# Hybrid decoder block on one core: a time mixer whose small matrix products are gathered into six runs a period in place of eight

## The chip, the core and the metric

The kernel runs on one core of a Trainium2 chip. Its engines run by themselves and meet only at semaphores: TensorE (PE, matrix products), VectorE (DVE), ScalarE (ACT), GpSimd (POOL), and SyncE (SP), which here only issues transfers. Each engine takes its instructions in the order in which they were written. The metric is the device time of one execution in microseconds; lower is better.

## What is computed

A decoder block on 256 tokens and 16 meta tokens, width 2048. One of its two token mixers is RWKV-7: 32 heads of 64, with a state S of 64x64 per head that runs over the tokens.

```
p = h @ w_in
r, k, v, wl, al, gl = split(shifted(p_rwkv))
decay = exp(-DECAY_SCALE * sigmoid(w0 + tanh(wl) @ w_w2))
a = sigmoid(a0 + al @ w_a2);  g = sigmoid(gl) @ w_g2
def step(S, inp):
    sa = S @ (-kk_t)
    S = S * w_t + sa (kk_t * a_t)^T + v_t k_t^T
    y_t = S @ r_t
y = (group_norm(y) + bonus) * g
```

The other mixer pools over windows. Both are merged by gates, projected, normalised, and followed by an expert stage (PEER) that gathers rows of two tables by index.

## The kernel before

The program is a row of stages, each a block in which all engines run: the front (norm, turning, the low-rank inputs), the time mixer `rwkv_stage`, `merge_stage`, the output product, and the expert stage. The change is in the time mixer alone.

The mixer works on pairs of heads (16 of them, 128 rows each) in a software pipeline written out by hand. Every engine runs the same table `ORDER` once a period, from the first entry to the last. An entry is a name and an index. The name is a unit of work, which an engine has or has not (`schedule` calls it only if its engine has it). The pair on which a unit works is the period's number less the unit's `STAGE`. So the table is the order of the instructions on PE, ACT and DVE at the same time; moving an entry moves it on all three.

The units:
- `f` n: n steps of the large projection of the next pair, each three products 128x128 by 272 columns (L197, `project`). 48 steps a period. `e` 0, 1, 2 take r, k and v out of PSUM. `sp` and `ahead` make the two parts (rounded and rest) of a weight half of 128x1024: ACT rounds (L161), DVE subtracts (L182). Eight steps of `f` use up one half.
- `lw`, `la`, `lg`: the low-rank products for decay, rate and gate (L645, L649, L654). `nm`, `bo`: sums over heads. All five write the same PSUM bank, `low_rank`, and each waits until the one before it has been taken out; for `lw` ACT does this by a tanh (L792), for `la` too (L797). On DVE `la` makes the running sum of the decay and mixes k.
- `gr`, `rb`, `t` 0 and 1: the products of the chunk matrices with each other, and their turning into token rows (`BKV_by_token`). DVE masks the results: `LT_diag`, `MT_st`, `RBKT_st`.
- `Z` i and `T` i, i from 1 to 5: the inverse of a triangular matrix per chunk, by doubling. `Z` multiplies `X_blocks` with `LT_diag` or `LT_off`, DVE masks (`Z_st`), `T` multiplies `Y_blocks` with `Z_st`, DVE adds into `Y_blocks` and transposes it into `X_blocks`. `T` 5 is the inverse's last product; DVE adds it into `Y_st`. `Z` 0 is DVE work only: three operations and the transpose.
- `r` c, `u` c, `s` c for the chunks c = 0 to 4: the scan. `r` makes the right-hand side (from chunk 1 on with the state `S`, in the product `chain<-S,A_st`), `u` multiplies with the inverse, `s` makes the new state, which DVE takes out as `S`. From chunk 2 on `r` also makes the output of the chunk before.
- `yc`, `gv`, `ge`, `gy`, `yf`, `ab`: the group norm of y, filling the inverse's other half, and the operands of the next pair.

The products of `gr`, `rb`, `t`, `Z`, `T`, `r`, `u` and `s` are made on 64x64 tiles of the array, for two heads at a time. They are called small here, and a stretch of them without any other product between is a run.

Of the kernel before, what the change touches and what calls it, by code (L numbers as in the profile page):

```python
# [18 lines left out]
T = META + SEQ  # L19
# [21 lines left out]
LEVELS = 6  # L41
# [42 lines left out]
class Core:  # L84
# [16 lines left out]
    def sb(self, name, shape, dt=F32, ctx=None, side="left", align=32):  # L101
        return (ctx or self.ctx).enter_context(self.nc.sbuf_tensor(name, shape, dt, side=side, align_bytes=align))
# [66 lines left out]
def wait(eng, sem, value):  # L169

    if not isinstance(value, int) or value > 0:
        eng.wait_ge(sem, value)
# [28 lines left out]
def front_stage(k, w):  # L201

    nc = k.nc
    with ExitStack() as ctx:
# [183 lines left out]
        def _(dve):  # L388
# [95 lines left out]


ORDER = (
# [11 lines left out]
)  # L498

STAGE = {"ahead": -1, "sp": 0, "cv": 0, "f": 0, "e": 0, "kn": 1, "lw": 1, "la": 1, "lg": 1, "ex": 1, "nm": 1, "nr": 1, "bo": 1, "ab": 1,  # L500
         "gr": 2, "rb": 2, "lo": 2, "Z": 2, "T": 2, "yf": 2, "t": 2,
         "r": 3, "u": 3, "s": 3, "yc": 3, "gv": 3, "ge": 3, "gy": 3}

WINDOWS_AT = ((1, 0), (1, 2))

# [5 lines left out]
def rwkv_stage(k, w):  # L511

    nc = k.nc
    with ExitStack() as ctx:  # L514
# [8 lines left out]
        r, kx, v = two("r", [P, TP]), two("k", [P, TP]), two("v", [P, TP])  # L523
# [15 lines left out]
        rhs, u, spc, s = sb("rhs", [P, CH]), sb("U", [P, CH]), sb("S_decayed", [P, CH]), two("S", [P, CH])  # L539
        yc, ysq, rstd = sb("y", [P, SEQ]), sb("y_square", [P, SEQ]), sb("y_rstd", [P, SEQ])  # L540
# [11 lines left out]
        q = {n: k.sem(f"r_{n}") for n in names}  # L552
# [18 lines left out]
        def by_head(out, wts, x, start=True, stop=True):  # L571

            for h in heads:
                mm = nc.tensor.matmul(out[h], wts[h], x[h], start=start, stop=stop)
            return mm
# [9 lines left out]
        def schedule(units):  # L585

            for b in range(-1, PAIRS + 3):
                for name, i in ORDER:
                    p = b - STAGE[name]
                    if name in units and 0 <= p < (PAIRS + 4 if name in STREAM else PAIRS):  # L590
                        units[name](i, p, p % 2)
# [24 lines left out]
        def _(pe):  # L616
            at, lead = [KT], [KT]

            def f(n, b, par):

                for _ in range(n):
                    if lead[0]:
                        lead[0] -= 1
                        continue
                    tile, kt = divmod(at[0], KT)
                    g, kh = divmod(at[0], HK)
                    if g == k.merge_at + GATES:
                        return
                    if kt == 0:
                        wait(pe, q["shifted"], tile - 1)  # L630
                    if kh == 0:
                        pe.wait_ge(k.s_split, g + 1)
                    t0 = META if g >= k.merge_at else 0
                    mm = product(nc, pr[tile % 2][:, 0:T - t0], (k.w_high[g % 3][:, kh, :], k.w_rest[g % 3][:, kh, :]),
                                 (k.hT_high[:, kt, t0:T], k.hT[:, kt, t0:T]), kt == 0, kt == KT - 1)
                    if kh == HK - 1:
                        mm.then_inc(k.s_used, 1)
                    at[0] += 1

            def lw(_, p, par):  # L640

                wait(pe, q["lora_w"], p * 48 + 48)
                wait(pe, q["tok"], p * 2)
                wait(pe, q["bonr"], p)
                nc.tensor.matmul(low[:, 0:T], ww2[:], k.lora[0:DECAY_LORA, 0, :], start=True, stop=True).then_inc(q["lora_mm"], 1)  # L645

            def la(_, p, par):
                wait(pe, q["sig"], p * 3 + 1)
                nc.tensor.matmul(low[:, 0:T], wa2[:], k.lora[0:ICL_LORA, 1, :], start=True, stop=True).then_inc(q["lora_mm"], 1)  # L649

            def lg(_, p, par):
                wait(pe, q["sig"], p * 3 + 2)
                for j in range(2):
                    mm = nc.tensor.matmul(low[:, 0:SEQ], wg2[:, j, :], k.lora[:, 2 + j, META:T], start=(j == 0), stop=(j == 1))  # L654
                mm.then_inc(q["lora_mm"], 1)
# [11 lines left out]
            def gr(_, p, par):  # L667

                wait(pe, q["st"], p + 1)
                wait(pe, q["kst"], p + 1)  # L670
                wait(pe, q["Y"], p * LEVELS)
                wait(pe, q["off"], p)
                for n, lhs in ((0, bst), (2, kst)):
                    for c in range(NCH):
                        mm = by_head(inv[n][:, c * CH:(c + 1) * CH], lhs[:, c, :], ast[par][:, c, :])
                    mm.then_inc(q["gram"], 1)

            def rb(_, p, par):
                wait(pe, q["rst"], p + 1)
                for n, lhs in enumerate((bst, kst)):  # L680
                    for c in range(1, NCH):
                        m = n * (NCH - 1) + c - 1
                        mm = by_head(inv[1][:, m * CH:(m + 1) * CH], lhs[:, c, :], rst[par][:, c, :])
                mm.then_inc(q["gram2"], 1)
# [70 lines left out]
            def gv(_, p, par):  # L755
                wait(pe, q["sqr"], p + 1)
                nc.tensor.matmul(var_ps, ones, ysq[:], start=True, stop=True).then_inc(q["var"], 1)

            schedule({"f": f, "lw": lw, "la": la, "lg": lg, "nm": nm, "bo": bo, "gr": gr, "rb": rb, "t": t,
                      "Z": Z, "T": T_, "r": r_, "u": u_, "s": s_, "gv": gv})  # L760
            f(2 * KT, PAIRS + 3, 0)

        @block.scalar
        def _(act):
# [17 lines left out]
            def kn_(_, p, par):  # L782
                wait(act, q["shifted"], p * 3 + 3)
                wait(act, q["st"], p)
                nc.scalar.activation(kn[:], kx[par][:], ACT.Copy, scale=cur[par][:, V_KK:V_KK + 1])
                wait(act, q["norm"], p)
                nc.scalar.activation(sq[:], kx[par][:], ACT.Square, scale=cur[par][:, V_KK:V_KK + 1]).then_inc(q["ksq"], 1)

            def lw(_, p, par):
                wait(act, q["csum"], p)  # L790
                wait(act, q["lora_mm"], p * 3 + 1)
                nc.scalar.activation(sg[:, real], low[:, 0:T], ACT.Tanh, scale=0.5, bias=cur[par][:, V_W0H:V_W0H + 1]).then_inc(q["sig"], 1)  # L792

            def la(_, p, par):
                wait(act, q["st"], p)
                wait(act, q["lora_mm"], p * 3 + 2)
                nc.scalar.activation(am[:, real], low[:, 0:T], ACT.Tanh, scale=0.5, bias=cur[par][:, V_A0H:V_A0H + 1]).then_inc(q["sig"], 1)  # L797
# [74 lines left out]
        def _(dve):  # L872
# [6 lines left out]
            def window(j):  # L879

                a, size, c0, at = k.pool_in[:, j, :], 1, 0, 0
                x = a
                d()
                while size < POOL_WINDOWS[j // 2]:
                    y = r[at]
                    n.tensor_tensor(y[:, c0 + size:T], x[:, c0 + size:T], x[:, c0:T - size], ALU.add)
                    d()
                    x, c0, size, at = y, c0 + size, 2 * size, 1 - at
                n.scalar_tensor_tensor(out=a[:, META:], in0=x[:, META:T], scalar=1.0 / POOL_WINDOWS[j // 2], in1=a[:, META:],
                                       op0=ALU.mult, op1=ALU.subtract)  # L890
# [135 lines left out]
            def gy(_, p, par):  # L1026
                if p == PAIRS - 1:
# [3 lines left out]

            wait(dve, q["zero"], n_zero)
            schedule({"ahead": sp_, "sp": sp_, "cv": cv, "e": e, "la": la, "nr": nr, "bo": bo, "ab": ab, "gr": gr, "rb": rb,
                      "Z": Z, "T": T_, "r": r_, "s": s_, "ge": ge, "gy": gy})
            window(6)
            for g in range(k.merge_at + 4, k.merge_at + GATES + 1):
                k.rest_half(dve, g)
# [946 lines left out]
```

## Time and profile before

| | us |
|---|---|
| median of 3 runs | 2472.08 |
| lowest and highest | 2471.37, 2472.72 |
| span of the profiled execution (first to last instruction) | 2469.5 |
| PE busy in it | 2193.7 |
| DVE busy | 1533.5 |
| ACT busy | 727.0 |

The profiled execution's own time outside its span is not given; its span stands 2.6 us below the median of the runs. Rows of the order of time have the start, the length from the first start to the last end, the engine, the line, the output and inputs, and how many neighbours of one kind were put together. In brackets stands idle time of the engine ahead of the row and what ended it. An instruction's length holds its pipeline too, so neighbours overlap; what one takes from the next is read from start to start. On PE the records of a product have two instructions per head or part, so a group of two products in the program stands as x4.

### The profile page before, as it was taken

The numbers are of one execution on the slowest core, as the hardware profiler recorded it, in microseconds if no ns is written. First come the engines' busy times: TensorE is split into PE (matmuls) and PEld (weight loads), VectorE is DVE, ScalarE is ACT, GpSimd is POOL, SyncE is SP. The second block draws the span as 40 slices with busy tenths as digits, with TensorE's granted clock in tenths as the row PEclk, the third lists the DMA queues.
The fourth block names the chain that finished last, engine by engine and source line by source line (L and its number), as shares of the span: only waits on it lengthen the run. The fifth ranks groups of instructions, "written<-read, shape, count | busy, mean of one in ns | idle before, by whom it ended". The sixth has DMA issues, their size and how long they took to land.

```text
span 2469.5 us, 39419 instructions
## 1 busy us (share of the span) xinstructions
PE 2193.7 (89%) x16183; PEld 1536.9 (62%) x16183; DVE 1533.5 (62%) x2579; ACT 727.0 (29%) x1383; POOL 664.8 (27%) x541
## 2 busy tenths in 40 slices
PE   7999999999999999999989888988787787777776
PEld 6899999999989999988644444533332232222222
DVE  7777777787764554456855776677445544444445
ACT  4555555555434444342211111111111000000000
POOL 1000000000000000002555545555545445444442
PEclk9999999999999999999999999999999999999999
DMA  5433333333347666484999999999999999999997
GB/s 198 137 94 86 100 88 89 97 90 86 97 120 224 184 187 182 139 303 181 404 420 423 423 426 427 427 427 428 427 427 427 426 427 427 427 427 427 427 427 290
DMA packets 346278, 708.29 MB, mean 287 GB/s; under 512 B 13834, under 2 KB 270434, under 8 KB 279778
## 3 DMA queue, kind: packets, MB, share of 16 engines
q0 software_dynamic: 74176, 537.01, 51.7%
q1 hardware_dynamic: 271684, 168.55, 23.3%
q8 instruction: 129, 2.11, 0.3%
q14 instruction: 49, 0.40, 0.0%
q10 hardware_dynamic: 240, 0.22, 0.0%
HBM read 703.63 MB, written 2.10 MB: 286 GB/s over the span
## 4 chain that ended last, share of the span: by engine, by line
DMA 33%; PE 15%; DVE 2%; issue 2%; POOL 1%; DVEq 0%; ACT 0%; POOLq 0%; ACTq 0%
DMA down_rows<-in_v_table,experts 25%; PE bank L1695 11%; DMA up_rows<-in_u_table,experts 8%; PE bank L1611 2%; POOL down_rows L1599 1%; DVE up_rows L1811 0%; PE bank L1638 0%; PE bank L1653 0%; PE bank L1659 0%; ACT diagonal L1755 0%; DVE one_hot L1251 0%; DVE expert_sides L1257 0%; PE bank L1621 0%; PE bank L1665 0%; DVE side_index L1230 0%
## 5 line engine op out<-in xcount | busy, mean ns | idle before, releaser
L1695 PE MATMUL bank<-down_rows,diagonal 128*128 128x512 f32 x2032 | 947.7, 611 | 210.7 <-DMA down_rows<-in_v_table,experts 173.1
L1811 DVE CUSTOM_DVE_ANT_0 up_rows<-up_rows,h 128x2048 f32<-128x2048 f32 x256 | 585.2, 2292 | 523.2 <-DMA up_rows<-in_u_table,experts 523.2
L1695 PEld LDWEIGHTS bank<-down_rows,diagonal 128*128 128x128 f32 x2032 | 375.2, 193 | 741.9 <-issue 385.7
L1593 POOL DMA_INDIRECT up_rows<-in_u_table,experts x256 | 286.0, 1117 | 1207.2 <-POOLq L1269 1091.4
L1599 POOL DMA_INDIRECT down_rows<-in_v_table,experts x256 | 370.3, 1446 | 523.5 <-PE bank L1695 510.5
L182 DVE TENSOR_TENSOR w_half_rest<-w_half,w_half_high 128x1024 fp32r<-128x1024 f32 x224 | 273.0, 1221 | 180.8 <-ACT w_half_high L161 178.9
L197 PE MATMUL project<-hT_high,w_half_high 128*128 128x272 f32 (+1 forms) x1152 | 353.5, 307 | 1.6 <-DVE r L909 1.3
L197 PE MATMUL project<-hT_high,w_half_rest 128*128 128x272 f32 (+1 forms) x1152 | 330.6, 287 | 0.0
L197 PE MATMUL project<-hT,w_half_high 128*128 128x272 f32 (+1 forms) x1152 | 330.0, 287 | 0.0
L161 ACT CAST w_half_high<-w_half 128x1024 fp32r<-128x1024 f32 x224 | 234.7, 1051 | 191.3 <-PE merge_ps L197 122.0
L197 PEld LDWEIGHTS project<-hT_high,w_half_high 128*128 128x128 f32 x1152 | 216.9, 188 | 11.3 <-DVE r L909 1.5
L1774 ACT ACTIVATE dots<-dots 128x4 f32<-128x4 f32 x64 | 13.3, 207 | 713.9 <-DVE dots L1811 713.9
L197 PEld LDWEIGHTS project<-hT,w_half_high 128*128 128x128 f32 x1152 | 217.0, 188 | 2.4
L197 PEld LDWEIGHTS project<-hT_high,w_half_rest 128*128 128x128 f32 x1152 | 216.9, 188 | 0.0
L1755 ACT ACTIVATE diagonal<-constants_kept,weights 128x128 f32<-128x128 f32 x256 | 82.3, 394 | 280.0 <-DVE weights L1818 280.0
L1611 PE MATMUL bank<-h1T,query_w 128*128 128x256 f32 x256 | 65.1, 388 | 10.2 <-ACT queryT L1720 10.2
L197 PE MATMUL merge_ps<-yaT_high,w_half_high 128*128 128x256 f32 x256 | 72.7, 284 | 1.4 <-PEq L514 1.4
L1611 PEld LDWEIGHTS bank<-h1T,query_w 128*128 128x128 f32 x256 | 49.5, 194 | 38.2 <-issue 33.8
L197 PE MATMUL merge_ps<-yaT_high,w_half_rest 128*128 128x256 f32 x256 | 72.4, 283 | 0.0
L197 PE MATMUL merge_ps<-yaT_rest,w_half_high 128*128 128x256 f32 x256 | 72.4, 283 | 0.0
L197 PE MATMUL merge_ps<-hT,w_half_high 128*128 128x256 f32 x256 | 72.1, 282 | 0.0
L197 PE MATMUL merge_ps<-hT_high,w_half_rest 128*128 128x256 f32 x256 | 72.0, 281 | 0.0
(338 smaller groups left out, 3013.2 us busy)
## 6 DMA issues: line engine op xcount, KB each, us to landing
w_half<-in_w_in SPq DMA_DIRECT2D x176, 512.0 KB, 4.0
w_half<-in_w_branch_a SPq DMA_DIRECT2D x32, 512.0 KB, 3.9
out_w<-in_w_out SPq DMA_DIRECT2D x16, 1024.0 KB, 5.3
query_w<-in_w_q_peer SPq DMA_DIRECT2D x10, 1024.0 KB, 19.7
w_half<-in_w_branch_b SPq DMA_DIRECT2D x16, 512.0 KB, 3.8
out_w<-in_w_q_peer SPq DMA_DIRECT2D x6, 1024.0 KB, 29.5
up_rows<-in_u_table,experts POOLq DMA_INDIRECT x256, 21.1
down_rows<-in_v_table,experts POOLq DMA_INDIRECT x256, 20.5
```

What stands on the lines that cost most here:

```text
L161: self.nc.scalar.copy(self.w_high[g % 3][:].bitcast(F32R), self.w_raw[g % 3][:]).then_inc(self.s_rounded, 1)
L182: return eng.tensor_tensor(low.bitcast(F32R), x, high, ALU.subtract)
L197: mm = nc.tensor.matmul(out, a.bitcast(F32R), b.bitcast(F32R), start=start and n == 0, stop=stop and n == 2)
L1593: pool.indirect_dma_start(ur[n % RU][:], None, w["u_table"][0], bass.IndirectOffsetOnAxis(ap=k.idx[:, t, h, j:j + 1], axis=0)).then_inc(s_ ...
L1599: pool.indirect_dma_start(vr[n % RV][:], None, w["v_table"][0], bass.IndirectOffsetOnAxis(ap=k.idx[:, t, h, j:j + 1], axis=0)).then_inc(s_ ...
L1611: mm = nc.tensor.matmul(pq[i][:, 0:SEQ], k.query_part(h, i, kt), k.h1T[:, kt, :], start=(kt == 0), stop=(kt == KT - 1))
L1695: mm = nc.tensor.matmul(acc[t][c][:], dg[n % RD][:], vr[n % RV][:, quarter(c)], start=(n == 0), stop=(n == last(t, c)), skip_group_check=True)
L1755: nc.scalar.activation(dg[n % RD][:], ident, ACT.Copy, scale=weights[:, n:n + 1]).then_inc(s_diag, 1)
L1774: nc.scalar.activation(x, x, ACT.Gelu).then_inc(s_gelu, 1)
L1811: v.tensor_tensor_reduce(ur[n % RU][:], ur[n % RU][:], k.h[:, n // (HEADS * TOPK), :], 1.0, 0.0, ALU.mult, ALU.add, dots[:, n:n + 1]).then ...
```

## The change

The table is rewritten. What was the eighth run (`T` 5 between two stretches of `f`) is now the entry `Tl` 5, first in the period after, where it joins the first run. `s` 0 leaves the first run; it opens a second one, which takes in `Z` 1, `r` 1, `t` 1, `T` 1 and `u` 1. `la` stands three steps of `f` behind `lw`. The steps of `f` are shared out anew, 48 as before. `gr` no longer waits for the end of the previous inverse but only for its fifth mask; `rb` has that wait.

```diff
 ORDER = (
-    ("r", 0), ("gr", 0), ("sp", 1), ("t", 0), ("rb", 0), ("u", 0), ("t", 1), ("Z", 0), ("s", 0), ("sp", 2), ("f", 2),
-    ("lw", 0), ("f", 4),
-    ("Z", 1), ("cv", 0), ("r", 1), ("f", 2),
-    ("la", 0), ("u", 1), ("T", 1), ("f", 7),
+    ("Tl", 5), ("r", 0), ("gr", 0), ("sp", 1), ("t", 0), ("rb", 0), ("u", 0), ("Z", 0), ("sp", 2), ("f", 6),
+    ("s", 0), ("Z", 1), ("cv", 0), ("r", 1), ("t", 1), ("T", 1), ("u", 1), ("lw", 0), ("f", 3), ("la", 0), ("f", 4),
     ("lo", 0), ("kn", 0), ("sp", 3), ("lg", 0), ("s", 1), ("Z", 2), ("r", 2), ("T", 2), ("u", 2), ("f", 3),
-    ("sp", 4), ("nm", 0), ("f", 2),
+    ("sp", 4), ("nm", 0), ("f", 3),
     ("s", 2), ("Z", 3), ("r", 3), ("nr", 0), ("T", 3), ("u", 3), ("f", 7),
-    ("s", 3), ("Z", 4), ("ex", 0), ("sp", 5), ("r", 4), ("T", 4), ("u", 4), ("bo", 0), ("f", 1),
+    ("s", 3), ("Z", 4), ("ex", 0), ("sp", 5), ("r", 4), ("T", 4), ("u", 4), ("bo", 0), ("f", 2),
     ("e", 0), ("s", 4), ("Z", 5), ("yc", 0), ("ab", 0), ("f", 2),
-    ("yf", 0), ("gv", 0), ("ge", 0), ("T", 5), ("f", 18),
+    ("yf", 0), ("gv", 0), ("ge", 0), ("f", 18),
     ("e", 1), ("ahead", 0), ("gy", 0), ("e", 2),
 )
...
-         "r": 3, "u": 3, "s": 3, "yc": 3, "gv": 3, "ge": 3, "gy": 3}
+         "Tl": 3, "r": 3, "u": 3, "s": 3, "yc": 3, "gv": 3, "ge": 3, "gy": 3}
...
                 wait(pe, q["st"], p + 1)
                 wait(pe, q["kst"], p + 1)
-                wait(pe, q["Y"], p * LEVELS)
+                wait(pe, q["Zst"], p * 5)
                 wait(pe, q["off"], p)
...
             def rb(_, p, par):
                 wait(pe, q["rst"], p + 1)
+                wait(pe, q["Y"], p * LEVELS)
```

On DVE, at the head of a period, this stood before (`w_half_rest` is the work of `sp` 2 here; `S` is the state after chunk 0):

```order
L954 TENSOR_TENSOR MT_st<-invert,constants 128x320
L182 TENSOR_TENSOR w_half_rest<-w_half,w_half_high 128x1024
L958 TENSOR_TENSOR RBKT_st<-invert,constants 128x512
L963 TENSOR_TENSOR Y_blocks<-LT_diag 128x160
L965 TENSOR_TENSOR Y_blocks<-Y_blocks,constants 128x160
L967 TENSOR_TENSOR Y_blocks<-Y_blocks,constants 128x160
L969 STREAM_TRANSPOSE X_blocks<-Y_blocks 128x160
L1006 TENSOR_SCALAR S<-chain,chunk_decay 128x64
L182 TENSOR_TENSOR w_half_rest<-w_half,w_half_high 128x1024
L975 TENSOR_TENSOR Z_st<-invert,constants 128x320
```

The same place on DVE after the change:

```order
L987 TENSOR_TENSOR Y_st<-Y_st,invert 128x4x32
L949 COPY chunk_decay<-decay_prod 128x5
L951 TENSOR_TENSOR LT_diag<-invert,constants 128x320
L953 TENSOR_TENSOR MT_st<-invert,constants 128x320
L182 TENSOR_TENSOR w_half_rest<-w_half,w_half_high 128x1024
L957 TENSOR_TENSOR RBKT_st<-invert,constants 128x512
L962 TENSOR_TENSOR Y_blocks<-LT_diag 128x160
L964 TENSOR_TENSOR Y_blocks<-Y_blocks,constants 128x160
L966 TENSOR_TENSOR Y_blocks<-Y_blocks,constants 128x160
L968 STREAM_TRANSPOSE X_blocks<-Y_blocks 128x160
L182 TENSOR_TENSOR w_half_rest<-w_half,w_half_high 128x1024
L1005 TENSOR_SCALAR S<-chain,chunk_decay 128x64
```

The inverse's last addition now stands ahead of the masks, and the weight half's rest ahead of `S` instead of behind it.

On PE, from the first state to the gate product, this stood before (the rows left out are large products: 6 ahead of the decay, 12 behind it, 6 ahead of the rate):

```order
L574 MATMUL chain<-U,BKV_by_token 64x64 x2
...
L645 MATMUL low_rank<-lora,w_decay 128x272
...
L574 MATMUL invert<-X_blocks,LT_diag 64x32 x10
L574 MATMUL chain<-BKV_by_token,MT_st 64x64 x2
L574 MATMUL chain<-S,A_st 64x64 x2
...
L649 MATMUL low_rank<-lora,w_rate 128x272
L574 MATMUL chain<-rhs,Y_st 64x64 x2
L574 MATMUL invert<-Y_blocks,Z_st 64x32 x10
```

The same stretch of PE after the change (left out are the 9 large products between decay and rate):

```order
L572 MATMUL chain<-U,BKV_by_token 64x64 x2
L572 MATMUL invert<-X_blocks,LT_diag 64x32 x10
L572 MATMUL chain<-BKV_by_token,MT_st 64x64 x2
L572 MATMUL chain<-S,A_st 64x64 x2
L572 MATMUL low_rank<-constants,V_st 64x64 x10
L572 MATMUL invert<-Y_blocks,Z_st 64x32 x10
L572 MATMUL chain<-rhs,Y_st 64x64 x2
L643 MATMUL low_rank<-lora,w_decay 128x272
...
L647 MATMUL low_rank<-lora,w_rate 128x272
```

The product with `S` now follows the making of that state with one `Z` and one small product between, and the rate follows the decay with nothing but nine large products between.

## Rows read from the trace of the kernel before

**Rows 1.** The page's head.

```profile
span 2469.5 us, 39419 instructions
```

**Rows 2.** Windows: busy us of each engine, granted clock, DMA share, GB/s.

```profile
577.48:614.89 37.41, 37.41 (x603) 34.56 (x602) 29.50 (x61) 21.97 (x42) 0.00 (x0) 1.00 0.34 93
...
690.00:724.00 34.00, 31.27 (x322) 28.80 (x320) 24.65 (x45) 11.27 (x20) 0.00 (x0) 1.00 0.40 110
```

**Rows 3.** Order of time on PE: a run of large products, and breaks.

```profile
561.82 0.29 PE L197 MATMUL project<-hT,w_half_high 128*128 128x272 f32 x1
...
564.21 0.29 PE L197 MATMUL project<-hT_high,w_half_rest 128*128 128x272 f32 x1
564.43 0.33 PE L574 MATMUL chain<-BKV_by_token 64*64 64x64 f32 x4
564.59 0.28 PE L574 MATMUL chain<-U,BKV_by_token 64*64 64x64 f32 x4
...
581.50 0.28 PE L574 MATMUL chain<-U,BKV_by_token 64*64 64x64 f32 x4
581.71 0.39 PE L197 MATMUL project<-hT_high,w_half_high 128*128 128x272 f32 x1
581.94 0.29 PE L197 MATMUL project<-hT,w_half_high 128*128 128x272 f32 x1
```

**Rows 4.** Order of time on PE: a period's head, its end, the next head.

```profile
577.48 0.33 PE L574 MATMUL chain<-BKV_by_token,MT_st 64*64 64x64 f32 x4
...
580.68 0.28 PE L574 MATMUL chain<-rhs,Y_st 64*64 64x64 f32 x4
...
606.79 0.59 PE L757 MATMUL chain<-y_square,constants 128*128 128x256 f32 x2
607.32 0.65 PE L574 MATMUL invert<-Y_blocks,Z_st 64*64 64x32 f32 x16
607.90 0.39 PE L197 MATMUL project<-hT_high,w_half_high 128*128 128x272 f32 x1
...
614.89 0.33 PE L574 MATMUL chain<-BKV_by_token,MT_st 64*64 64x64 f32 x4
```

**Rows 5.** Decay and rate: order of time on PE and ACT, and line 792.

```profile
582.55 0.62 PE L645 MATMUL low_rank<-lora,w_decay 96*128 96x272 f32 x2
...
583.26 1.28 ACT L792 ACT_TABLE_LOAD   x1 [0.29 <-PE low_rank L645]
584.55 0.49 ACT L792 ACTIVATE decay_sigmoid<-low_rank,pair_vectors 128x272 f32<-128x272 f32 x1
...
586.43 0.62 PE L649 MATMUL low_rank<-lora,w_rate 96*128 96x272 f32 x2
...
L792 ACT ACT_TABLE_LOAD  x13: 1283/1283/1283, 171.7 to 620.7; - x13
```

**Rows 6.** Order of time on DVE: border and head; a later rest and state.

```profile
577.18 1.23 DVE L182 TENSOR_TENSOR w_half_rest<-w_half,w_half_high 128x1024 fp32r<-128x1024 f32 x1 [0.44 <-ACT w_half_high L161]
...
578.66 0.49 DVE L909 SCALAR_TENSOR_TENSOR v<-project,pair_vectors,v 128x271 f32<-128x271 f32 x1
...
581.07 0.69 DVE L958 TENSOR_TENSOR RBKT_st<-invert,constants 128x512 f32<-128x512 f32 x1
...
583.06 0.35 DVE L969 STREAM_TRANSPOSE X_blocks<-Y_blocks 128x160 f32<-128x160 f32 x1
...
595.71 1.23 DVE L182 TENSOR_TENSOR w_half_rest<-w_half,w_half_high 128x1024 fp32r<-128x1024 f32 x1 [1.02 <-ACT w_half_high L161]
597.05 0.28 DVE L1004 SCALAR_TENSOR_TENSOR S<-chain,chunk_decay,S_decayed 128x64 f32<-128x64 f32 x1
```

**Rows 7.** Second state: rounding on ACT, then two groups on PE.

```profile
588.96 1.05 ACT L161 CAST w_half_high<-w_half 128x1024 fp32r<-128x1024 f32 x1
...
591.51 0.33 PE L574 MATMUL chain<-BKV_by_token 64*64 64x64 f32 x4
...
592.49 0.28 PE L574 MATMUL chain<-S,A_st 64*64 64x64 f32 x4
```

More of the change, by code:

```diff
@@ L759, in _ @@
             schedule({"f": f, "lw": lw, "la": la, "lg": lg, "nm": nm, "bo": bo, "gr": gr, "rb": rb, "t": t,
-                      "Z": Z, "T": T_, "r": r_, "u": u_, "s": s_, "gv": gv})
+                      "Z": Z, "T": T_, "Tl": T_, "r": r_, "u": u_, "s": s_, "gv": gv})
             f(2 * KT, PAIRS + 3, 0)
@@ L1033, in _ @@
             schedule({"ahead": sp_, "sp": sp_, "cv": cv, "e": e, "la": la, "nr": nr, "bo": bo, "ab": ab, "gr": gr, "rb": rb,
-                      "Z": Z, "T": T_, "r": r_, "s": s_, "ge": ge, "gy": gy})
+                      "Z": Z, "T": T_, "Tl": T_, "r": r_, "s": s_, "ge": ge, "gy": gy})
             window(6)
```

## Prediction

> **What bounds the kernel now.** I read four views: the page, the windows of single periods of the time mixer, the order of time on TensorE (PE), and the order of time on VectorE (DVE) and ScalarE (ACT) beside it. The span is 2469.5 us [rows 1]; the median of the runs is 2472.08, so some 2.6 us lie outside it, and I add my difference to the median. In the mixer a period lasts 37.41 us, and PE is busy for all of it at a granted clock of 1.00, while DVE has 29.5 us of work [rows 2]. So in this stage every microsecond added to PE's row of work, or in which it stands, is a microsecond of the end. The stages behind it start when it ends and I let them move as one. The question is therefore only this: what does PE save on breaks between small and large products, and does it now stand anywhere?
>
> **What the breaks cost.** Inside a run of large products one starts every 0.126 us: 19 steps from 561.82 to 564.21. The first small (64x64 tile) group follows the last large one by 0.22 instead of 0.126, and the second group follows after 0.16 instead of 0.12. Back again, the large product comes 0.21 after the last small group instead of 0.12, and is itself followed after 0.23 instead of 0.126 [rows 3]. One round trip thus costs 0.095 + 0.04 + 0.09 + 0.105 = 0.33 us. (The full-array products of lw, la, nm, bo and gv are no such break; they pay by their columns.) The change has 6 round trips a period in place of 8: **-0.66 us a period**. Some 16 periods have the inverse in them, so the most that the change can give is about -11 us. The Trainium skill (TensorEngine Tiling (Array Packing), Key Properties) says that changing the tiling mode drains TensorE. The trace agrees, with the 0.33 us above. By that rule alone the change would only be faster; that is the first rival.
>
> **First wait: S of the first chunk.** I count from the first small group of a period. The inverse's last product has left the previous period, so this point comes earlier by what it took there: 0.58 from its start to the next product, and the breaks, 0.77 in all [rows 4]. DVE's work at the border does not come earlier: the rounding rest that stands ahead of it (577.18) waits for ACT, whose work hangs on the y chain that starts at the fifth level (Z5), the same distance back. So in the new count that row stands at -0.30 + 0.77 = +0.47. From there RBKT starts 3.89 later, plus about 0.2 for the inverse's last addition, which now stands ahead of the masks: 4.56. The transpose that Z1 needs starts 1.99 later and lasts 0.35: Z1 can start at 6.95. Then, by the new order, the third half's rest (1.23) goes ahead of S instead of behind it. It starts at about 6.85, S starts 1.34 after it (as 595.71 to 597.05) and ends at 8.47 [rows 6]. PE meanwhile: the last product 0.53, then 3.16 to u0 (577.48 to 580.68, less the entry), 0.21 to the six large ones, 0.23 + 16 x 0.126 + 0.22 for them: s0 starts at 6.37 [rows 3, 4]. From the start of s to the product with S it is 0.98 when nothing waits (591.51 to 592.49) [rows 7], so S is wanted at 7.35 and there at about 8.5: **+1.15 us**. Before, six large products, lw, and two more stood between s0 and the product with S, and hid all this. Bounds: if the border work did come earlier by the 0.77, the wait is 0.4; if another 0.3 of DVE work stands in the way, 1.45. I take 1.15 since the row at 577.18 itself shows idle time that ends with ACT.
>
> **Second wait: la behind lw.** Both write `low_rank`, and la must wait until ACT has taken the tanh out of it. lw starts at 582.55; the table load for tanh starts only after it, at 583.26, takes 1.28, and the tanh ends at 585.04: 2.49 us after the start of lw. Before, six large products and a run of small ones lay between (la at 586.43). Now it is three: 0.46 for lw and 9 x 0.126 make 1.59. PE stands for **0.9 us** (0.05 of handing over makes it 0.95). The load is there in 13 periods only [rows 5]; without it the tanh ends 2.49 - 1.28 = 1.2 after the start of lw and nothing waits. The Trainium skill (ScalarE: Activation LUTs, Rules for kernel authors) would budget about 2.7 us for a change of table set; by that this wait alone would be 2.3 us and the time some 18 us above my sum. The row has 1.283 us, 13 times over, and decides.
>
> **Third wait: S of the second chunk.** From la to s1 it was 5.08 (586.43 to 591.51). The run u1, T1 (about 0.85 and its two breaks, 0.2) and three of the seven large products (1.13) have gone from between: 2.9. S is wanted 0.98 later, at la + 3.9. What sets S is not PE: DVE first does la's own chain and then the rest of the fourth half, which waits for ACT's rounding. ACT does rate, LT_off, k and its square, and starts rounding 2.53 after la (588.96), 2.44 without the copy of U that now comes sooner; it ends at 3.5. Rest and S by the same 1.34, S itself 0.28: la + 5.15 [rows 5 to 7]. **+1.3 us**, where before there was room. Bounds: 0.9 if DVE gets the rounding 0.4 sooner; 1.5 if the copy of U still stands there. The second and third waits follow one another and add up, since the chain of the third starts at la.
>
> **What costs nothing.** t1 moved between r1 and T1: it is the same 20 products, it covers T1's mask, and its eviction ends a little before lw wants `low_rank` (some 0.15 of room; if that is gone, 0.1 to 0.2 a period). gr without its wait for the inverse's end: rb has it instead, 2.2 us later on PE, and the addition on DVE (at about 2.4 to 2.7) is just there. The rest of the period keeps its distances; two large products moved into it from other places only give more cover. SP's weight loads keep their order.
>
> **The sum.** 1.15 + 0.9 + 1.3 - 0.66 = +2.7 a period, so 40.1 us for 37.41. This holds for the 13 periods with table load, all other stages being filled: +35. The first period with a scan has neither the load nor the y chain before it: +1. The one before it, and the last two, which have no lw and la and where the change also removes a wait ahead of T5, give about -2. Together **+34 us: 2506**.
>
> **Rivals.**
> (a) The waits are hidden and only the breaks count: -11, 2461. It needs the three waits together under 0.66 a period. Against it is the 1.28 us load, which alone is longer than three products. 5%.
> (b) Only la waits, DVE being early enough otherwise: 13 x 0.9 - 11 = +1, 2473. DVE has 7.9 us idle a period, but it lies in other places. 6%.
> (c) The border work comes earlier with PE and the first wait is 0.4: -0.75 x 14, 2496. 14%.
> (d) A further wait appears, at lw for the eviction, at Z1, or at rb: +0.5 a period, 2513. 13%.
> (e) The granted clock falls in the new gaps. In 690 to 724 PE was busy for 92% of the time at 1.00 [rows 2], and I forecast 93%; 2%, with a time far above all these.
> My own case: 60%, with 2501 to 2511 for it.
>
> **The numbers.** The range for 8 in 10 takes in (c) and (d): 2492 to 2518. A measurement of this kernel tells 0.2% (5 us) from no change. Faster has (a): 0.05. Same has (b) in most of its width: 0.05. Slower has the rest: 0.90.
>
> **What would show it.** Periods of about 40.1 us; PE idle time ended by S (the tensor_scalar and the scalar_tensor_tensor) of some 1.1 and 1.3 us, and one of 0.9 ended by ACT's tanh ahead of `w_rate`; la 2.5 us after lw in place of 3.9; 96 products first in a row after small groups in place of 128. I am wrong if PE's idle time in a period is below 2 us, or if the period has another wait of over 0.5 us; the most doubtful step is where DVE stands at the border.

## The result and the profile after

The changed kernel takes 2521.97 us (median of 4 runs, 2516.01 to 2525.53) against 2471.86 for the kernel before; the ratio is 1.0199 (95% interval 1.0185 to 1.0213). It is slower by 50 us. The forecast had the sign, at 2506, and its range ended at 2518: the time lies 4 us outside it. In these four runs each the kernel before repeats within 1.4 us, the changed one spreads over 9.5. Over more runs the difference is smaller: in experiment 10 the same changed kernel spreads over 3.5 us (4 runs), and the kernel before over 5.2 (15 runs).

The head of the page of the changed kernel, to be set beside [rows 1]; its execution took 2518.87 us.

```profile
span 2516.9 us, 39434 instructions
```

Windows of the changed kernel, from one `LT_diag` on DVE to the next, which is one period (columns as in [rows 2]). The first two are ordinary periods, the third is not; the last three cut a piece out of it.

```profile
456.85:497.25 40.40, 37.89 (x610) 35.08 (x608) 29.69 (x62) 21.93 (x42) 0.00 (x0) 1.00 0.32 85
497.25:537.66 40.41, 37.90 (x610) 35.09 (x608) 29.70 (x63) 21.94 (x42) 0.00 (x0) 1.00 0.31 86
619.11:660.88 41.77, 39.28 (x610) 36.36 (x608) 29.68 (x63) 21.93 (x42) 0.00 (x0) 0.96 0.30 83
634.00:636.00 2.00, 1.64 (x41) 1.48 (x41) 1.14 (x4) 0.21 (x1) 0.00 (x0) 0.89 0.54 136
636.00:638.00 2.00, 2.00 (x11) 2.00 (x10) 0.46 (x2) 0.21 (x1) 0.00 (x0) 0.50 0.69 201
638.00:640.00 2.00, 2.00 (x12) 1.72 (x12) 0.53 (x1) 1.59 (x2) 0.00 (x0) 0.76 0.02 6
```

The reader is to see two things. An ordinary period lasts 40.40 us in place of 37.40, with PE idle for 2.5 of them, where it was never idle before. And now and then a period lasts 1.4 us more, and in it the granted clock falls to 0.50 (1.2 of 2.4 GHz).

The waits of PE in the changed kernel from 200 to 660 us, 11 periods and a bit (us in total, times, longest):

```profile
PE chain L572 <- DVE S L1003: 11.7, 11, 1.1
PE low_rank L647 <- ACT decay_sigmoid L791: 8.6, 11, 0.8
PE chain L572 <- DVE S L1005: 6.3, 11, 0.6
```

They are the three waits of the forecast (`L1003` is the second chunk's `S`, `L1005` the first one's). The order of time on PE through such a stretch, that of 619 to 661 us:

```profile
623.09 0.28 PE L572 MATMUL chain<-U,BKV_by_token 64*64 64x64 f32 x4
623.44 0.77 PE L572 MATMUL invert<-X_blocks,LT_diag 64*64 64x32 f32 x20
624.04 0.31 PE L572 MATMUL chain<-BKV_by_token,MT_st 64*64 64x64 f32 x4
624.93 0.33 PE L572 MATMUL chain<-S,A_st 64*64 64x64 f32 x4 [0.57 <-DVE S L1005]
...
626.47 0.72 PE L643 MATMUL low_rank<-lora,w_decay 96*128 96x272 f32 x2
...
629.11 0.73 PE L647 MATMUL low_rank<-lora,w_rate 96*128 96x272 f32 x2 [0.78 <-ACT decay_sigmoid L791]
...
632.99 0.31 PE L572 MATMUL chain<-BKV_by_token,MT_st 64*64 64x64 f32 x4
634.36 0.33 PE L572 MATMUL chain<-S,A_st 64*64 64x64 f32 x4 [1.07 <-DVE S L1003]
...
636.34 0.43 PE L197 MATMUL project<-hT,w_half_high 128*128 128x272 f32 x1
636.57 0.43 PE L197 MATMUL project<-hT_high,w_half_rest 128*128 128x272 f32 x1
```

From start to start, less the 0.12 to 0.15 that such a step takes when nothing waits: 0.23 for the transpose ahead of Z1, 0.75 for the first S, 1.23 for the second. From decay to rate it is 2.64, where 1.59 is work: 1.05. (The number in brackets is smaller than the loss, since it counts from the modelled end of the product before.) The last two rows show the clock's fall: large products 0.23 apart instead of 0.126. What the three waits hang on, on ACT and DVE in the same stretch:

```profile
623.31 1.18 DVE L182 TENSOR_TENSOR w_half_rest<-w_half,w_half_high 128x1024 fp32r<-128x1024 f32 x1
624.59 0.28 DVE L1005 TENSOR_SCALAR S<-chain,chunk_decay 128x64 f32<-128x64 f32 x1
...
627.28 1.28 ACT L791 ACT_TABLE_LOAD   x1 [0.48 <-PE low_rank L643]
628.57 0.49 ACT L791 ACTIVATE decay_sigmoid<-low_rank,pair_vectors 128x272 f32<-128x272 f32 x1
...
631.64 1.04 ACT L161 CAST w_half_high<-w_half 128x1024 fp32r<-128x1024 f32 x1
632.70 1.23 DVE L182 TENSOR_TENSOR w_half_rest<-w_half,w_half_high 128x1024 fp32r<-128x1024 f32 x1 [0.21 <-ACT w_half_high L161]
634.02 0.28 DVE L1003 SCALAR_TENSOR_TENSOR S<-chain,chunk_decay,S_decayed 128x64 f32<-128x64 f32 x1
```

Each S comes straight behind a rest of 1.2 us, and the tanh behind its load, as in [rows 5, 6] but now with nothing on PE to cover them.

A fourth wait stands once in the whole run, behind the ordinary periods. From the last `LT_diag` to the first product of the merge stage, first in the kernel before, then in the changed one (columns as in [rows 2]):

```profile
653.54:724.28 70.74, 65.82 (x886) 60.86 (x882) 48.65 (x96) 23.57 (x48) 0.00 (x0) 1.00 0.38 106
700.82:774.72 73.90, 65.80 (x868) 61.49 (x865) 48.55 (x96) 23.49 (x47) 0.00 (x0) 0.98 0.37 101
```

The same work takes 3.2 us longer. In the changed kernel PE and DVE have there:

```profile
734.14 0.65 PE L572 MATMUL invert<-Y_blocks,Z_st 64*64 64x32 f32 x16
738.16 0.48 PE L572 MATMUL chain<-rhs,Y_st 64*64 64x64 f32 x4 [3.23 <-DVE Y_st L987]
...
734.29 0.43 DVE L900 COPY pool_in<-project 128x272 f32<-128x272 f32 x1
...
737.39 0.42 DVE L888 SCALAR_TENSOR_TENSOR pool_in<-r,pool_in 128x256 f32<-128x256 f32 x1
737.74 0.28 DVE L987 TENSOR_TENSOR Y_st<-Y_st,invert 128x128 f32<-128x128 f32 x1
```

The inverse's last product is done before 735, but its addition stands on DVE behind the pooling steps, which fill 734.29 to 737.8, and `u` 0 needs it. In the kernel before the addition stood ahead of them, and large products came between:

```profile
683.78 0.28 DVE L988 TENSOR_TENSOR Y_st<-Y_st,invert 128x128 f32<-128x128 f32 x1
683.98 0.44 DVE L901 COPY pool_in<-project 128x272 f32<-128x272 f32 x1
...
688.78 0.33 PE L574 MATMUL chain<-rhs,Y_st 64*64 64x64 f32 x4 [0.31 <-ACT rhs L831]
```

In each of the experiments that has `Tl` 5 at the head of the period PE stands 3.2 us at this place.

### The profile page after: what moved, and what is told of

It is laid out like the page before. It is cut to its first block, busy times and chain, and to the rows that moved or that the text cites. A ratio compares the mean times of both kernels' runs of the same rounds, so it can differ in the third digit from the quotient of the medians.

```text
span 2516.9 us, 39434 instructions
## 1 busy us (share of the span) xinstructions
PE 2202.4 (88%) x16183; PEld 1545.5 (61%) x16183; DVE 1536.4 (61%) x2579; ACT 725.7 (29%) x1383; POOL 663.5 (26%) x541
## 4 chain that ended last, share of the span: by engine, by line
DMA 32%; PE 14%; DVE 2%; issue 2%; POOL 1%; DVEq 0%; ACT 0%; POOLq 0%; ACTq 0%
DMA down_rows<-in_v_table,experts 25%; PE bank L1694 11%; DMA up_rows<-in_u_table,experts 8%; PE bank L1610 2%; POOL down_rows L1598 1%; DVE up_rows L1810 0%; PE bank L1652 0%; PE bank L1658 0%; PE bank L1637 0%; ACT diagonal L1754 0%; DVE one_hot L1250 0%; DVE expert_sides L1256 0%; PE bank L1620 0%; DVE side_index L1229 0%; DVE side_index L1222 0%
```

## The experiments

In what follows a period is an ordinary one, read between two `LT_diag` rows; a fall is a stretch at half clock, of about 3.4 us each in the windows. Falls are counted in one profile of each kernel. A diff of `ORDER` shows only the pieces of its lines that differ. The profile of the changed kernel has five, at 110, 147, 270, 636 and 738 us. That of the kernel before has none between 90 and 750 us. The last of the five follows the wait for `Y_st`.

**1. The tanh table loaded early.** On ScalarE (its tile and its name in the list of units are left out):

```diff
+            def cv(_, p, par):
+                nc.scalar.activation(warmed[:], eps[:], ACT.Tanh)
```

> The changed kernel, but ScalarE computes one tanh of a single column at entry cv, so that its table is loaded while it idles (3.6 us there), and the tanh of lw no longer has 1.28 us of load ahead of it. Theory of three waits: the 0.94 us that PE stands ahead of la go, and all that hangs on la's start comes that much earlier: 13 x 0.94 = 12 us less, period 39.5 instead of 40.4, median about 2508, and less again if the clock falls less often. Rival (the wait at la is only the place where time is lost that is then lost at S): the wait goes to S, no gain, 2520.

Measured: 2513.73 (2507.71 to 2517.97), ratio 1.0178 (1.0161 to 1.0195). Period 39.33 to 39.35, which is 1.06 less; the wait ahead of the rate is gone from PE's list, the two for S are as they were. ScalarE's row now has the tanh right behind the product:

```profile
457.50 0.49 ACT L795 ACTIVATE decay_sigmoid<-low_rank,pair_vectors 128x272 f32<-128x272 f32 x1 [0.49 <-PE low_rank L644]
```

The wait was its own loss and moved nowhere. The median gained 8 us, less than 13 x 1.06 = 14, and this kernel too has five falls, four of them ahead of 700 us.

**2. The third half's rest behind Z1.**

```diff
-("Z", 0), ("sp", 2), ("f", 6),
-("s", 0), ("Z", 1), ("cv", 0),
+("Z", 0), ("f", 6),
+("s", 0), ("Z", 1), ("sp", 2), ("cv", 0),
```

> The changed kernel with entry sp 2 behind Z 1 instead of ahead of s 0, so that on DVE the rest of the third half (1.23 us) stands behind S of the first chunk and behind the mask. Theory of three waits: PE's wait for S (0.75 us from start to start) goes, that for the transpose ahead of Z1 (0.23) stays: 14 x 0.75 = 10 us less, median about 2510. Rival: the rest then delays the addition and the second S and the time is only moved: 2520.

Measured: 2508.72 (2507.32 to 2513.24), ratio 1.0158 (1.0142 to 1.0175). Period 39.60, 0.79 less. The waits for `S L1005` are gone. As the theory had it. Three falls come ahead of 700 us.

**3. The fourth half behind u2.**

```diff
-("lo", 0), ("kn", 0), ("sp", 3), ("lg", 0), ("s", 1), ("Z", 2), ("r", 2), ("T", 2), ("u", 2), ("f", 3),
+("lo", 0), ("kn", 0), ("lg", 0), ("s", 1), ("Z", 2), ("r", 2), ("T", 2), ("u", 2), ("sp", 3), ("f", 3),
```

> The changed kernel with entry sp 3 behind u 2 instead of behind kn, so that ScalarE's rounding and DVE's rest of the fourth half stand behind the S of the second chunk. Theory of three waits: the wait of 1.24 us for that S goes: 14 x 1.2 = 17 us less, about 2504; if the large gaps are also what brings the clock down, some 5 more. Rival: the half then comes too late for its products 24 on, and a wait for split appears there; 2515 or more.

Measured: 2498.25 (2497.12 to 2499.81), ratio 1.0112 (1.0095 to 1.0129). Period 39.18, 1.21 less, and only two falls, both behind 710 us. The median gained 24 us where 14 periods give 17; the falls that are gone would account for most of the rest (1.4 us each).

**4. All three.**

> The changed kernel with all three mends (tanh table loaded early, sp 2 behind Z 1, sp 3 behind u 2). Theory of three waits and a clock that falls only because of them: period 40.4 - 0.94 - 0.75 - 1.24 = 37.5, no stretch of the mixer at a clock under 1.00, median about 2472, even with the kernel before. Rival 1 (the breaks gain the full 0.66 a period once nothing waits): 36.8 a period, 2462. Rival 2 (the clock falls for another reason): 2480, with the falls still there.

Measured: 2474.88 (2471.82 to 2476.41), ratio 1.0012 (1.0003 to 1.0022), over 10 runs. Windows of its period and of most of the mixer:

```profile
429.18:466.53 37.35, 37.25 (x610) 34.85 (x608) 29.60 (x62) 22.27 (x43) 0.00 (x0) 1.00 0.34 93
90.00:700.00 610.00, 600.90 (x9581) 562.19 (x9580) 469.31 (x949) 340.05 (x656) 0.00 (x0) 1.00 0.34 92
```

The period is 3.04 shorter; the three mends apart gave 1.06 + 0.79 + 1.21 = 3.06. So the three waits are separate and add up, and with them gone the kernel is back within 3.5 us of the one before. One fall is left, at 691 us, in the wait for `Y_st`. What this does not explain is why two breaks less are worth nothing then; experiments 6, 11 and 12 take that up.

**5. La later, the same steps.**

```diff
-("lw", 0), ("f", 3), ("la", 0), ("f", 4),
+("lw", 0), ("f", 6), ("la", 0), ("f", 1),
```

> The changed kernel with six steps of f between lw and la and one behind la, instead of three and four. The tanh then has 0.46 + 18 x 0.126 = 2.73 us, so PE does not stand ahead of la. Theory (the second and third wait are one chain lw, tanh, la, rate, rounding, rest, S): la starts when it did, S comes when it did, and the wait for S grows from 1.2 to about 2.2: no change of the period (40.4), 2520. Rival (each wait is its own): 0.94 a period less, 2508.

Measured: 2534.47 (2531.73 to 2539.90), ratio 1.0259 (1.0242 to 1.0276). The ordinary period is 40.46 to 40.47, unchanged, and the loss ahead of the second S is 1.98 - 0.14 = 1.84 instead of 1.23, with another 0.26 idle ahead of the gate product. So the chain from the decay to the second S is one chain: moving large products about inside it gains nothing. But the time rose by 12 us at an unchanged ordinary period. Two neighbouring periods show where:

```profile
424.95:465.42 40.47, 37.87 (x610) 35.06 (x608) 29.68 (x62) 21.94 (x42) 0.00 (x0) 1.00 0.31 86
465.42:507.29 41.87, 39.26 (x610) 36.42 (x608) 29.69 (x62) 21.94 (x42) 0.00 (x0) 0.96 0.30 82
```

Same work, same idle time, 1.4 us apart, by the clock alone. Between 90 and 800 us this profile has about 41 us at half clock, that of the changed kernel 17. The idle time of a period is hardly larger (2.60 us for 2.51), only more of it is in one place: the wait for the second `S` is 1.68 us in the rows instead of 1.07.

**6. The inverse's last product moved, nothing else.** The kernel before with `("Tl", 5)` at the head of the period, its waits in `gr` and `rb`, and no `("T", 5)`.

> The kernel before with one part of the change alone: T 5 goes to the head of the next period (with its waits in gr and rb), all else as before: seven runs. Theory: one break less is 0.33 us x 16 = 5 us less, and DVE, 0.77 late at the head, still has room ahead of S: 2467, period 37.1. Rival (the late head costs by itself): a wait for S or the transpose of 0.3 or more, 2472 or slower.

Measured: 2469.66 (2468.88 to 2471.78), ratio 0.9996 (0.9987 to 1.0006). Period 37.21, 0.19 less than before. In the PE rows the tail from `gv` to the next head is 0.78 shorter (7.32 for 8.10) and the head from its first group to u0 0.54 longer (3.74 for 3.20), of which 0.05 is `rb` standing for the addition. A break is thus worth some 0.29, the move 0.19 to 0.24, and the late head costs nothing where S has room. The total is no measurable change, and the profile shows why: from the first `LT_diag` to the last it is 2.2 us shorter than the kernel before (556.54 for 558.72), but from the last one to the merge stage 1.7 longer (72.46 for 70.74), since PE stands 3.22 us for `Y_st` there and the clock falls.

**7. The change without that move.** The changed kernel with `("T", 5)` back between `gv` and the 18 steps.

> The changed kernel with T 5 back at its old place between gv and the 18 steps: seven runs. Theory: one break more (+0.33), but DVE is no longer 0.77 late at the head, so the wait for the transpose (0.23) and most of that for S (0.75, then about 0.2) go; waits at la and the second S stay. Period 40.4 + 0.33 - 0.75 = 40.0, about 2515. Rival (head not late because of the moved product): 40.7, 2526.

Measured: 2518.47, the median of three executions (2516.74 to 2519.34), ratio 1.0186 (1.0166 to 1.0206); a fourth took 5885 us, which nothing here explains, and is left out. Period 40.19, 0.2 less than with the move. The loss at the transpose (0.23) is gone, that at the first S went from 0.75 to 0.60. So I was half right: the late head makes 0.38 of the 0.98 at this place, and the greater part is the rest that stands ahead of S.

**8. The gaps filled with work.** In the changed kernel PE multiplies where it would stand, with results that nobody reads:

```diff
+            def fill(n, b):
+
+                g, kh = divmod(at[0], HK)
+                wait(pe, q["shifted"], 3 * b)
+                for _ in range(n):
+                    nc.tensor.matmul(pr[1 - at[0] // KT % 2][:, 0:SEQ], k.w_high[g % 3][:, kh, :].bitcast(F32R), k.hT_high[:, kh, META:T].bitcast(F32R), start=True, stop=True)
...
             def la(_, p, par):
+                if 3 <= p:
+                    fill(7, p + 1)
```

and 3 and 7 in `r` of the chunks 1 and 2.

> The changed kernel with products that nobody reads (128x128 by 256 columns, into the project bank that is free then) put where PE would stand: 7 ahead of la, 3 and 7 ahead of the products that wait for S. It adds work and leaves the waits as long as they were. Theory (the clock falls because PE stands, and costs what the profile shows at half clock): no stretch of the mixer under 1.00, period 40.4 as before, time 7 to 12 us under the changed kernel's 2522, that is 2510 to 2514, and runs that agree within 1 us. Rival (clock not tied to the gaps): 2522 or more, spread of 9 us as before.

Measured: 2554.77 (2551.95 to 2556.70), ratio 1.0339. This run does not test the theory, by a mistake of mine: `fill` waited for `v` at the head of every period even for no products, and PE stood there instead:

```profile
PE chain L572 <- DVE v L919: 21.7, 11, 2.3
```

The three old gaps had gone from its list and a new one of up to 2.3 us was there, and the clock fell more often than in the changed kernel (31 us at half clock between 90 and 800 us, in nine falls). Eight of them come in or behind that new gap, which is at least a hint.

**9. The same, mended, and 10. the changed kernel beside it on the same chip.** `fill` returns at once if n is 0.

> As the fill kernel before it, mended: that one also waited at the head of every period for v of the last tile, even where it filled nothing (2.3 us of standing a period). Now the wait stands only where something is filled, where v has long been done. PE works through the three gaps (7, 3 and 7 products that nobody reads), which stay as long as they were. Theory (the clock falls where PE stands): no stretch of the mixer between 130 and 700 us under a clock of 1.00, regular period 40.4 to 40.6, median 2508 to 2516, runs within 2 us of each other. Rival (the clock falls for another reason, such as the mix of products): falls as often as in the changed kernel (5 in its profile), 2520 or more.

> The changed kernel itself, on the same chip as the fill kernel, so that the two can be set side by side. Both theories: 2516 to 2526, four to seven falls of the clock in its profile, regular period 40.4.

Measured: filled 2516.16 (2514.49 to 2517.20), ratio 1.0182 (1.0167 to 1.0198); unfilled 2522.27 (2520.72 to 2524.21), ratio 1.0208 (1.0192 to 1.0223). An ordinary period is 40.40 in both. Windows of the filled kernel, one period and most of the mixer:

```profile
453.93:494.33 40.40, 40.31 (x627) 37.40 (x624) 29.68 (x62) 21.94 (x42) 0.00 (x0) 1.00 0.31 86
90.00:700.00 610.00, 605.16 (x9284) 561.81 (x9284) 446.38 (x899) 323.96 (x616) 0.00 (x0) 1.00 0.31 86
```

and of the unfilled one:

```profile
90.00:700.00 610.00, 572.43 (x8930) 530.07 (x8929) 441.17 (x888) 321.24 (x611) 0.00 (x0) 0.99 0.31 85
```

With 17 products more a period, and the waits of DVE and ACT just as long, the kernel is 6.1 us faster. Up to 700 us there is no fall, against four in the unfilled one; the spread is 2.7 us, against 3.5. From the first `LT_diag` to the last it is 601.02 us against 606.39, 5.4 less, about four falls of 1.4. So the clock falls because PE stands, and that is a part of the loss by itself. It also shows that PE's own time was never the matter here: three waits of 3 us together are the 3 us of the period. The one fall that the filled kernel has, at 733 us, stands in the wait for `Y_st`, where nothing was filled.

**11. The steps shared out as before.** The changed kernel with only this:

```diff
-("la", 0), ("f", 4),  ...  ("nm", 0), ("f", 3),  ...  ("bo", 0), ("f", 2),
+("la", 0), ("f", 6),  ...  ("nm", 0), ("f", 2),  ...  ("bo", 0), ("f", 1),
```

> The changed kernel with only the steps of f shared out otherwise: six behind la instead of four, two behind nm instead of three, one behind bo instead of two, as in the kernel before. Theory: from la to s 1 it is 0.76 us longer, so the wait for S of the second chunk falls from 1.24 to about 0.5; half 1 is used up two steps sooner, so its place in ScalarE's row is free as early as in the kernel before and the wait of 0.20 for the third S, which the prediction did not have, goes. Period 40.4 - 0.76 - 0.2 = 39.4, median 2506 to 2510. Rival (the third S waits for something else): the 0.20 stays, 39.6 a period, 2512.

Measured: 2502.71 (2500.72 to 2503.99), ratio 1.0133 (1.0116 to 1.0149). Period 39.47, 0.93 less. The second S costs 0.62 - 0.14 = 0.48. The third S, for which the changed kernel has 0.34 from start to start (517.76 to 518.10 in its rows) instead of 0.15, has 0.15 again. Three figures in a table are worth 19 us, falls included (two instead of five).

**12. Six runs without waits.** All three mends, the fourth half's rounding at its old place and only its rest later, and:

```diff
+    ("Tl", 5), ("r", 0), ("gr", 0), ("sp", 1), ("t", 0), ("rb", 0), ("u", 0), ("Z", 0), ("f", 7),
+    ("s", 0), ("Z", 1), ("sp", 2), ("cv", 0), ("r", 1), ("t", 1), ("T", 1), ("u", 1), ("lw", 0), ("f", 4), ("la", 0), ("f", 4),
+    ("lo", 0), ("kn", 0), ("sp", 3), ("lg", 0), ("s", 1), ("Z", 2), ("rest", 3), ("r", 2), ("T", 2), ("u", 2), ("f", 3),
+    ("sp", 4), ("nm", 0), ("f", 2),
...
+    ("s", 3), ("Z", 4), ("ex", 0), ("sp", 5), ("r", 4), ("T", 4), ("u", 4), ("bo", 0), ("f", 1),
```

> The six runs with their waits taken out: tanh table loaded early; the rest of the third half behind Z 1; the rest of the fourth half behind Z 2 on DVE, its rounding where it was; seven steps of f ahead of s 0 (covers the transpose, 0.23), four between lw and la (covers 0.11), two behind nm and one behind bo as in the kernel before (so that half 1 is used up as early as there, which takes away 0.20 at the third S). Theory: no wait over 0.1 a period, so the two breaks saved remain: 37.4 - 0.6 = 36.8 a period, 14 periods, no falls: 2462 to 2464. Rival (the breaks are worth less than their rows, since with three mends the period was still 37.35): 37.2 or more, 2469.

Measured: 2467.41 (2465.50 to 2468.91) over 11 runs against 2470.81 (2467.91 to 2473.06), ratio 0.9986 (0.9977 to 0.9995).

```profile
425.17:462.09 36.92, 36.92 (x610) 34.70 (x608) 29.45 (x62) 22.15 (x43) 0.00 (x0) 1.00 0.35 93
```

The period is 0.48 shorter than before and PE never idle in it. Over 14 periods that would be 7 us; 3.4 are measured. In the profile the kernel gains 5.5 us from the first `LT_diag` to the last (553.20 for 558.72) and 0.6 ahead of them, and loses 2.8 from there to the merge stage (73.55 for 70.74), where PE stands 3.24 us for `Y_st` and two falls come, at 682 to 690. That makes 3.4. An order in which the inverse's last addition stands ahead of the pooling steps in that one period was not tried.

## Why the prediction was right and wrong

**What bounds it** was right: experiment 9 gave PE 17 products more a period and the time fell.

**The breaks** were priced at -0.66 a period for two. Measured: 0.29 for one in experiment 6, and experiment 12 is 0.48 under the kernel before with about 0.05 lost in `rb`. Right in kind, about a fifth too high. The Trainium skill's rule that I set beside it (TensorEngine Tiling (Array Packing), Key Properties), a drain at a change of tiling mode, fits the rows of the changed kernel too: its first small group starts 0.22 behind the last large product (622.71 to 622.93), where large ones follow one another by 0.126.

**First wait**, +1.15: 0.98 (0.23 and 0.75). Right. The reason given for it, the late head, makes 0.38 of this, the rest ahead of S the remainder; both were in the sum. (4.56 + 1.99 + 0.35 is 6.90 and not 6.95, which moves nothing.)

**Second wait**, +0.9 to 0.95: 1.05, and experiment 1 takes 1.06 away by loading the table early. Right. The load is 1.28 in the trace after, 13 times, and the tanh starts as it ends (627.28 + 1.28 to 628.57), so the 2.7 us of the Trainium skill (ScalarE: Activation LUTs, Rules for kernel authors) for a change of set are not seen here either.

**Third wait**, +1.3: 1.23. Right, and experiment 5 shows that it and the second are one chain, as I had put it. (Its terms add up to la + 5.11, not 5.15.)

**"Two large products moved into it from other places only give more cover"** was wrong. The steps moved to places behind nm and bo were taken from ahead of s1. So half 1 was used up two steps later, ScalarE's rounding of the fifth half waited for it (1.10 us for `project` at 515.36, where the kernel before has 0.35), DVE's rest for that, and the third S for DVE: 0.2 a period, gone in experiment 11. Together with the second wait and the breaks this makes the period 40.40 where the sum gave 40.1: 13 x 0.3 = 4 us, or 13 x 0.37 = 5 by the profile of the filled kernel.

**The last two periods** were put at a gain, in a term of -2 us with the period ahead of the scan. From the last `LT_diag` to the merge stage they need 73.90 us in the changed kernel, 73.92 in the filled and 74.02 in the unfilled one, against 70.74: a loss of 3.2, so the term was some 4 to 5 us too low. What failed there is that the forecast looked only at the wait ahead of `T` 5, which the move takes away (0.68), and not at what stands on DVE ahead of the addition at its new place: the pooling steps, and behind them PE for 3.23 us. A fall in this wait is part of the 3.2. Less these 3.2 us the time would be 2518.8, still 1 us outside the range.

**Rival (e), the clock,** is the largest step that failed. I gave it 2%, since in 690 to 724 "PE was busy for 92% of the time at 1.00" [rows 2]. An ordinary period of the changed kernel has about the same mean busy share (94%), but in other pieces; a mean says nothing of how the idle time lies. The longest wait of PE in 690 to 724 is 0.8 us (for `S L1004`); in the changed kernel PE waits 1.07 us for the second S, and behind it the clock falls in some periods and not in others, 1.4 us each time. I had also priced it wrongly, as "far above all these"; it is 6.1 us here (experiments 9 and 10). Without it the time would be 2516, in the range. How much of the spread of the runs comes with it is not shown: from the start of the merge stage to the end the profiles differ by up to 3.7 us (1742.2 to 1745.9), whatever the order in the mixer.

**The point** was therefore low by 16 us, by 17.5 for the pair of experiments 9 and 10 (51.5 over the kernel before beside it). Of these, 6 are clock, 4 to 5 the period, 4 to 5 the last two periods, and some 2 the first two periods of the inverse: the filled kernel has them 0.4 and 2.1 us longer, where I had put a gain into the first and 1 on the second.

## What to carry to other kernels

When work is gathered into longer runs, what lay between was cover: write down for every result that another engine makes how long it takes and what PE does meanwhile, before the pieces are moved. Steps of a stream that look alike are not free to move either; each eighth one here lets a buffer go, and a buffer let go late is a wait three steps on. And follow each moved result through the last periods, where other work stands between the entries: here its addition came behind pooling steps, 3.2 us, in every kernel that had the move. Prefer to move what is late (a table load, the rest of a weight half) ahead of or behind the chain; that brought 3.06 us a period, and moving the large products inside it nothing.

## What the runs showed of the hardware

A stretch of the mixer whose mean is over 90% busy can still see the granted clock fall to 0.50, behind single waits of PE. The profiles from 90 to 680 us, one of each kernel (a stretch of 6.8 us at half clock counts as two falls):

| longest wait of PE in an ordinary period, by the rows | kernels | falls up to 680 us |
|---|---|---|
| 1.07 us (second S) | changed, its repeat (10), experiments 1, 2, 7 | 4, 4, 4, 3, 3 |
| 1.68 us (second S) | 5 | 10 |
| 1.94 to 2.3 us (`v`) | 8 | 8 |
| 0.8 us (`w_rate`) | 3, 11 | none, none |
| under 0.3 us | before, 4, 6, 9, 12 | none |

All but two of these falls begin less than 2 us from the end of that longest wait; the two, at 110 us in the changed kernel and 112 in experiment 5, come in the same way at a wait for `Z_st` of 1.47 and 2.08 us in the first period. It does not take three waits close together: experiments 1 and 2 have only two of the three, with the last of them whole, and the falls stay; experiments 3 and 11 keep the first two and take the last away or shorten it to 0.31, and the falls go. With the same idle time a period but more of it in one place (5) there are far more, and with the waits filled by useless products none. In the last period of the scan a wait of 3.2 us (12 profiles, all with `Tl`) or 2.4 us (experiment 7, for `S`) always had a fall with it. Each fall lasted about 3.4 us at 0.50 and cost 1.4 in an ordinary period. Which periods it hits changed from run to run.
